# Expert loop: output weights fetched one expert ahead into a staging place and copied on by the vector engine

## The reference, cut to what matters

```python
def expert_block(args):
    xi, e = args
    hc = xi @ w1[e] + b1[e]                 # w1[e]: 1024 x 2048
    g, u = hc[:, :D_EXPERT], hc[:, D_EXPERT:]
    g = jnp.minimum(g, SWIGLU_LIMIT)
    u = jnp.clip(u, -SWIGLU_LIMIT, SWIGLU_LIMIT)
    hm = (u + 1.0) * (g * jax.nn.sigmoid(SWIGLU_ALPHA * g))
    return hm @ w2[e] + b2[e]               # w2[e]: 1024 x 1024
```

## Time and profile before

| | us |
|---|---|
| median of three runs | 2389.04 |
| the three runs | 2378.5, 2389.04, 2397.48 |
| the profiled execution | 2383.9 |
| its span | 2382.0 |
| PE busy | 2081.7 (87%) |
| DVE busy | 981.0 (41%) |
| ACT busy | 553.4 (23%) |
| POOL busy | 500.0 (21%) |
| DMA mean over the span | 329 GB/s |

### The profile page before, as it was taken

How to read it: one execution, slowest core, us unless ns; L and a number is a source line. 1 busy time by engine, 2 the same in 40 slices (tenths; PEclk the granted TensorE clock), 3 DMA queues, 4 the chain that set the end, 5 groups by cost and what they waited for, 6 DMA issues and landing times.

```text
span 2382.0 us, 27251 instructions
## 1 busy us (share of the span) xinstructions
PE 2081.7 (87%) x9038; PEld 1177.1 (49%) x9039; DVE 981.0 (41%) x2273; ACT 553.4 (23%) x1024; POOL 500.0 (21%) x562
## 2 busy tenths in 40 slices
PE   8998998957668577675899989999999999999998
PEld 7777887623223233232578854444444444444443
DVE  5955556547566566554275232211111111111112
ACT  4636301212112112121214222211111111112112
POOL 0000002466666666666200000000000000000000
PEclk9999999988788788897999989999999999999999
DMA  7352487799999999998743429799999999999996
GB/s 301 142 212 70 189 357 266 262 377 351 367 364 372 359 377 356 379 353 340 291 181 113 167 96 382 294 429 428 428 429 428 428 429 428 428 429 428 428 429 280
DMA packets 111703, 784.34 MB, mean 329 GB/s; under 512 B 13056, under 2 KB 13312, under 8 KB 80160
## 3 DMA queue, kind: packets, MB, share of 16 engines
q1 hardware_dynamic: 37920, 515.18, 52.2%
q0 software_dynamic: 73728, 268.47, 29.7%
HBM read 782.55 MB, written 1.05 MB: 329 GB/s over the span
## 4 chain that ended last, share of the span: by engine, by line
PE 71%; issue 12%; DVE 6%; POOL 3%; ACT 3%; DMA 2%; another core or an unknown queue 2%; DVEq 1%; POOLq 0%; ACTq 0%; SPq 0%
PE ps L779 57%; PE ps L938 11%; DVE ring L1932 2%; DMA arena<-in_peer_v,arena 2%; PE ps L1201 1%; POOL ring L739 1%; POOL ring L737 1%; PE ps L911 1%; DMA ring<-in_peer_v,arena 1%; ACT arena L1269 1%; DVE arena L1932 1%; DVE arena L1690 1%; DVE arena L1687 0%; DVE arena L1881 0%
## 5 line engine op out<-in xcount | busy, mean ns | idle before, releaser
L779 PE MATMUL ps<-ring,arena 128*64 128x512 f32 (+2 forms) x3336 | 749.6, 589 | 41.7 <-issue 41.7
L779 PEld LDWEIGHTS ps<-ring,arena 128*64 128x64 f32 (+1 forms) x3336 | 263.1, 140 | 501.2 <-issue 500.6
L938 PE MATMUL ps<-ring,arena 128*128 128x512 f32 x768 | 377.7, 649 | 147.3 <-issue 102.0
L779 PE MATMUL ps<-arena,ring 128*128 128x256 f32 (+1 forms) x2272 | 489.7, 375 | 3.8 <-DVE arena L1675 3.2
L779 PEld LDWEIGHTS ps<-arena,ring 128*128 128x128 f32 x2272 | 420.2, 190 | 66.7 <-issue 7.3
L938 PEld LDWEIGHTS ps<-ring,arena 128*128 128x128 f32 x768 | 157.8, 209 | 362.7 <-issue 309.2
L1932 DVE CUSTOM_DVE_ANT_0 ring<-ring,ps 128x1024 f32<-128x1024 f32 x192 | 228.6, 1218 | 105.9 <-DMA ring<-in_peer_v,arena 100.6
L938 PE MATMUL ps<-arena 128*128 128x512 f32 (+2 forms) x600 | 207.1, 594 | 69.9 <-ACT arena L1269 65.4
L1590 ACT COPY arena<-ps 128x512 f32<-128x512 f32 (+1 forms) x165 | 89.1, 540 | 739.7 <-PE ps L779 683.5
L2244 DVE TENSOR_TENSOR arena<-ps,arena 128x512 f32<-128x512 f32 x66 | 45.7, 692 | 438.7 <-PE ps L1201 438.7
L779 PE MATMUL ps<-arena 128*128 128x128 f32 (+4 forms) x1502 | 216.0, 299 | 9.3 <-ACT arena L1253 6.5
(11 more groups left out here) (336 smaller groups left out, 1214.8 us busy)
## 6 DMA issues: line engine op xcount, KB each, us to landing
ring<-in_w_exp SPq DMA_DIRECT2D x192, 2048.0 KB, 17.1
ring<-in_w_in SPq DMA_DIRECT2D x24, 2048.0 KB, 9.7
ring<-in_w_ada SPq DMA_DIRECT2D x12, 2048.0 KB, 9.0
ring<-in_w_out SPq DMA_DIRECT2D x4, 2048.0 KB, 8.4
ring<-in_w_peer_q SPq DMA_DIRECT2D x4, 2048.0 KB, 10.7
ring<-in_w_br_rnn SPq DMA_DIRECT2D x4, 1280.0 KB, 7.5
ring<-in_w_br_attn SPq DMA_DIRECT2D x2, 2048.0 KB, 14.3
ring<-in_peer_u,arena POOLq DMA_INDIRECT x192
```

The source lines that it names most:

```text
L779: return pe.matmul(o, l, r, start=start, stop=stop)
L938: return pe.matmul(o, l, r, start=start, stop=False, skip_group_check=True)
```

## The change

Ring and arena become two parts of one SBUF tensor (`words`), so that one instruction can address either by a register. Two staging places are laid over memory that is dead once the second block's `h3r` transposes are done. The output weights of expert e+1 are fetched into the staging places during expert e, each half under a semaphore of its own (`s_moved`), and the vector engine copies each half from staging to the ring after D of the pass before has been read. For a second pass of one expert the source is the ring place itself (`from_staged` holds 0), so that the copy moves data onto itself. Expert 0's output weights are loaded directly, expert 1's are staged before the loop. TensorE's D waits for the copy. After the loop the vector engine waits for the last copies. The units of the ring change their places (`place_of`), so that output weights lie at both ends.

```diff
--- before.py
+++ after.py
@@ -337,9 +337,9 @@
         def sem(name):
             return ctx.enter_context(nc.semaphore(name))
 
-        ring = ctx.enter_context(nc.sbuf_tensor("ring", [P, 6 * SLOT], F32))
         arena_words = 27400
-        arena = ctx.enter_context(nc.sbuf_tensor("arena", [P, arena_words], F32))
+        words = ctx.enter_context(nc.sbuf_tensor("words", [P, 6 * SLOT + arena_words], F32))
+        ring, arena = words[:, 0:6 * SLOT], words[:, 6 * SLOT:]
         ps = ctx.enter_context(nc.psum_tensor("ps", [P, N_BANKS, 512], F32))
         at = {"fixed": 0}
 
@@ -360,6 +360,7 @@
         ones = carve("fixed", P)
         cols = carve("fixed", N_COLS)
         eps = carve("fixed", 2)
+        staged_at = 6 * SLOT + at["fixed"]
         xT = carve("fixed", KD, T)
         hT = carve("fixed", KD, T)
         rstd = carve("fixed", T)
@@ -504,13 +505,19 @@
         of_pass = carve("M", 2, P)
         expert_of, part_of = of_pass[:, 0, :], of_pass[:, 1, :]
         last_of = carve("M", E)
+        from_staged = carve("M", P)
         assert at["M"] <= at["B"]
         g2_diag = carve("B", KD, P)
         assert at["B"] <= kept, (at["B"], kept)
         y_rows = ring[:, 0:TT * D].rearrange("p (a b) -> p a b", b=D)
         I32 = mybir.dt.int32
-        w1_unit = [ring[:, n * SLOT:(n + 1) * SLOT].rearrange("p (c j) -> p c j", c=KD) for n in range(4)]
-        w2_unit = [ring[:, n * SLOT:(n + 1) * SLOT].rearrange("p (c j) -> p c j", j=D) for n in (4, 5)]
+        place_of = {4: 0, 0: 1, 1: 2, 2: 3, 3: 4, 5: 5}
+        unit_words = [ring[:, place_of[n] * SLOT:(place_of[n] + 1) * SLOT] for n in range(6)]
+        w1_unit = [unit_words[n].rearrange("p (c j) -> p c j", c=KD) for n in range(4)]
+        w2_unit = [unit_words[n].rearrange("p (c j) -> p c j", j=D) for n in (4, 5)]
+        w2_start = [place_of[n] * SLOT for n in (4, 5)]
+        w2_staged = [words[:, staged_at + start:staged_at + start + SLOT] for start in w2_start]
+        assert at["M"] <= staged_at + w2_start[1] - 6 * SLOT <= kept - SLOT
 
         s_par = sem("params_loaded")
         s_x = [sem(f"x_loaded_{j}") for j in range(4)]
@@ -627,6 +634,7 @@
         s_g, s_sg = sem("expert_gate_ready"), sem("expert_sigmoid_ready")
         s_hm = sem("expert_hidden_ready")
         s_yg = sem("expert_rows_ready")
+        s_moved = [sem(f"staged_weights_moved_{half}") for half in range(2)]
         s_fin = sem("experts_done")
         s_y, s_yroot, s_yn = sem("y_ready"), sem("y_root_ready"), sem("y_normed")
         s_row = sem("rows_loaded")
@@ -664,9 +672,15 @@
                     sp.wait_ge(s_poolB, 1)
                     sp.dma_start(b2[0:E, :], a["b_exp_out"]).then_inc(s_smallw, 16)
 
-            def load(e, n):
-                sp.dma_start(ring[:, n * SLOT:(n + 1) * SLOT],
+            def load(e, n, to=None):
+                sp.dma_start(unit_words[n] if to is None else to,
                              a["w_exp"][bass.ds(e, 1), n].rearrange("e p w -> (e p) w")).then_inc(w_full[n], 16)
+
+            def stage(e, q=None):
+                for half in range(2):
+                    if q is not None:
+                        sp.wait_ge(s_moved[half], q + 2)
+                    load(e, 4 + half, w2_staged[half])
 
 
             n_second = len(units)
@@ -675,16 +689,25 @@
                     sp.wait_ge(s_mrg, 4 + 4)
                     load(0, 5)
                 unit_free(sp, last_in_slot(n, n_second))
-                load(0, n)
+                load(0, next(u for u in range(6) if place_of[u] == n))
+            B.filled(sp, "h3r", 3)
+            stage(1)
             sp.wait_ge(s_slots, 1)
             sp.dma_start(final_row, a["final_g"].partition_broadcast(P)).then_inc(s_row, 16)
-            with sp.Fori(1, E) as e:
-
-                q = sp.value_load(last_of[0:1, bass.ds(e - 1, 1)].bitcast(I32), min_val=0, max_val=MAX_PASSES - 1)
-                for job, ns in (("Zg", (0, 1)), ("Zu", (2, 3)), ("D", (4, 5))):
+            def last_pass(e):
+                return sp.value_load(last_of[0:1, bass.ds(e, 1)].bitcast(I32), min_val=0, max_val=MAX_PASSES - 1)
+
+            def first_weights(e, q):
+                for job, ns in (("Zg", (0, 1)), ("Zu", (2, 3))):
                     X.filled(sp, q, job)
                     for n in ns:
                         load(e, n)
+
+            with sp.Fori(1, E - 1) as e:
+                q = last_pass(e - 1)
+                first_weights(e, q)
+                stage(e + 1, q)
+            first_weights(E - 1, last_pass(E - 2))
             for t in range(TT):
                 sp.wait_ge(s_yn, t + 1)
                 sp.dma_start(out[t * P:(t + 1) * P, :], y_rows[:, t, :]).then_inc(s_out, 16)
@@ -1236,6 +1259,7 @@
                 for k in range(KD):
                     if k % 4 == 0:
                         pe.wait_ge(w_full[4 + k // 4], e * 16 + 16)
+                        pe.wait_ge(s_moved[k // 4], q + 1)
                     for half in range(2):
                         last = mm(ps[half * NS:(half + 1) * NS, EXPERT_BANK["D"], :],
                                   hm[:, k % 4, (k // 4) * NS:(k // 4 + 1) * NS],
@@ -2214,7 +2238,10 @@
                     own(dve.tensor_copy(last_of.bitcast(I32), count))
                 elif kind == "table":
                     B.filled(dve, *job)
-                    own(dve.tensor_copy(of_pass[0:E].rearrange("p a b -> p (a b)").bitcast(I32), ps[0:E, b, 0:2 * P]))
+                    own.mark(dve.tensor_copy(of_pass[0:E].rearrange("p a b -> p (a b)").bitcast(I32),
+                                             ps[0:E, b, 0:2 * P]))
+                    own(ts(from_staged[0:E], ps[0:E, b, P:2 * P], 0.5, float(staged_at), ALU.is_lt, ALU.mult))
+                    own(dve.tensor_copy(from_staged[0:E].bitcast(I32), from_staged[0:E]))
                     dve.sem_inc(free[b], 1)
                     dve.sem_inc(s_slots, 1)
                 elif kind == "gT":
@@ -2228,11 +2255,14 @@
             own(dve.tensor_copy(bias_now, b1[:, 0, :]))
             select(selg, 0, 0, True)
             dve.sem_inc(s_selg, 1)
+            for half in range(2):
+                dve.sem_inc(s_moved[half], 1)
             total = dve.value_load(total_i[0:1, 0:1].bitcast(I32), min_val=E, max_val=MAX_PASSES)
             with dve.Fori(0, total) as q:
                 own.enter(q, 2 + 6 + 1 + 2 + 1)
                 e = dve.value_load(expert_of[0:1, bass.ds(q + 1, 1)].bitcast(I32), min_val=0, max_val=E - 1)
                 part = dve.value_load(part_of[0:1, bass.ds(q + 1, 1)].bitcast(I32), min_val=0, max_val=3)
+                source = dve.value_load(from_staged[0:1, bass.ds(q + 1, 1)].bitcast(I32), min_val=0, max_val=staged_at)
                 dve.wait_ge(s_xg, q * 2 + 2)
                 select(sel, e, part, False)
                 dve.sem_inc(s_sel, 1)
@@ -2262,12 +2292,18 @@
                 own(tt(yg, ps[:, EXPERT_BANK["D"], :], g2_halves, ALU.mult))
                 dve.sem_inc(x_free[EXPERT_BANK["D"] - 4], 1)
                 dve.sem_inc(s_yg, 1)
+                for half in range(2):
+                    dve.wait_ge(w_full[4 + half], e * 16 + 16)
+                    dve.tensor_copy(unit_words[4 + half], words[:, bass.ds(source + w2_start[half], SLOT)])\
+                        .then_inc(s_moved[half], 1)
                 own.leave_open()
             end = Own(dve, s_vend)
 
 
             dve.wait_ge(s_fin, 1)
             dve.wait_ge(s_row, 16)
+            for half in range(2):
+                dve.wait_ge(s_moved[half], total + 1)
             halves = lambda x: x.rearrange("p (a b) -> p a b", b=512)
             end(tt(halves(y_rows[:, 1, :]), ps[:, 2:4, :], halves(final_row), ALU.mult))
             dve.sem_inc(s_y, 1)
```

## The result

The change made the kernel slightly slower, by less than one per cent: 2399.8 us in the median of 20 runs against 2390.98 of 20 runs before, ratio 1.0043 with a 95% interval of 1.0028 to 1.0058, which is 7 to 14 us. The forecast was 2395 (range 2377 to 2409), 6.35 us above before.

What follows compares the result with a forecast made beforehand. The expert loop was taken as bound by DMA bytes due before the last Zu. Terms 3.2 (later issue), 0.5 (front) and 2.65 (tail) sum to 6.35 us, on the median 2389.04 giving 2395 us, range 2377 to 2409.

Steps and rivals of the forecast that it cites:

- What bounds: Expert loop: DMA saturated at 428 GB/s, passes 29.36 us apart; the wait ending last is before Zu, not D.
- The count of bytes: From the DMA restart to u(31)'s landing: 28 output-weight pairs before and after, net 0 us where 9.8 could be expected.
- Rival A: Fetching ahead is worth one pair's transfer: loop ends 9.8 us sooner, whole time 2382 us; chance 0.12.
- The issue of w2: Output weights issued 3.2 us later, behind product and copy; paid once, at the first saturated expert, +3.2 us.
- The vector engine's time: Two copies a pass, 4.8 us with gaps, and a register load fit into 12.58 us of idle time: 0 us.
- In front of the loop: Two small vector operations before the signal that starts the loop: +0.5 us, bounds 0 and 0.8.
- The tail: After the last pass the final product waits for needless copies, 2.9 us later; a 0.25 us wait falls away: +2.65 us.
- Sum: Whole kernel: 3.2 + 0.5 + 2.65 = 6.35 us above the kernel before.
- Rival B: Each vector copy runs at the slow rate, 4.44 us, adding 12.9 us: 2402 us; chance 0.12.
- Rival C: Copies and arriving weights hold each other up, decisive once a pass's first copy takes over 5.8 us; slower; chance 0.05.
- price of a restart: When a dry DMA queue restarts, 0.54 us lost in the microsecond after the issue at 1525.33, at 197 GB/s.

Runs made afterwards that it cites:

- alternate: Changed kernel without copies, odd experts' output weights used where staged; ratio to the kernel before 1.0008, time from end of expert 0's Zu 952.75 us.
- direct_last: Changed kernel with the last expert's output weights loaded straight to the ring; ratio to the kernel before 1.0005, time from end of expert 0's Zu 957.31 us.
- switch_25: As alternate, but from expert 26 on output weights go out behind their own expert's other weights; ratio to the kernel before 0.9958.
- copy_thrice: Changed kernel with two further same-size copies ahead of each copy; time from end of expert 0's Zu 1070.44 us, 109 us above the change.
- skip_last: Changed kernel without the two copies of the last pass; time from end of expert 0's Zu 959.08 us, 2.4 us less than the change.
- copy_twice: Changed kernel with one further same-size copy ahead of each copy; time from end of expert 0's Zu 1009.39 us, 48 us above the change.

## Why the prediction was right

**What bounds.** Right. The wait stays before Zu and the saturated rate at 428 GB/s; the spacing of passes is 29.38 instead of 29.37. The DMA ends as the last Zu starts, as forecast (table of stretches, then timeline):

```profile
2362.00:2363.00 1.00, 0.00 (x0) 0.00 (x0) 0.00 (x0) 0.59 (x1) 0.00 (x0) 1.00 0.05 16
```
```profile
2363.49 7.09 PE L802 MATMUL ps<-words 128*64 128x512 f32 x32 [1.49 <-issue]
```

**The count of bytes, 28 pairs against 28, worth 0.** Right, and shown by alternate, which pays for no copies and gains 1.2. My reason for it was incomplete. I named the last Zu's bytes; direct_last took a pair out of that count and gained 1.8, not 9.8. The full reason is that before every Zu in the saturated loop the same number of bytes is due, and TensorE's own 27.64 us cap what any lead can give back per pass. Rival A's gain exists (switch_25 has 8.0 of the 9.8 us), but only for a kernel that gives the lead up five or six passes before the end.

**The issue of w2.** The size was nearly right, 3.46 instead of 3.2 (the gap before the copy is 0.42, not 0.26). The step that failed is the word once, "But once, at the first saturated expert". The same delay counts a first time at expert 2: the queue was dry after u(1), w2(2) stands ahead of g(2) and u(2), and u(2) misses its Zu. That pass is 1.6 us longer (29.25 against 27.64). Of the 3.46 us by which w2(2) goes out later, 1.9 are absorbed and 1.6 reach TensorE. The second pass of expert 2, from which my count started, lets the DMA catch up but gives TensorE nothing back.

**The vector engine's time.** Right: copies of 2.29 us, and no wait of TensorE for them in the changed kernel. In copy_thrice, with six copies a pass, the cover is used up.

**In front of the loop.** 0.4 measured, 0.5 expected.

**The tail.** 2.63 measured, 2.65 expected, shown by skip_last (2.4).

**Sum.** 0.4 + 1.6 + 3.5 + 2.63 = 8.1 us where 6.35 stood. The missing part is the term at expert 2. The medians differ by 8.8, the ratio gives 10.3 with an interval from 6.7 to 13.9, which holds 8.1 but not 6.35. The measured 2399.8 lies 4.4 us above the forecast of 2395.4: 1.9 because the median of 20 runs before is higher than that of the three that I had, 1.8 from the missing term, and the rest is within the scatter. The number held because the missing term is small against the range (2377 to 2409); the mechanism was right but for this one place.

**Rival B** is refuted by the copy's 2.29 us. **Rival C** did not come, since weights land at full rate beside the copies; but its threshold, a first copy of 5.8 us, was too high: two copies in a row, 4.6 us, already suffice. Its price of a restart, 0.54 us, was too low: copy_twice loses 2.55 at the one shown.

## What to carry to other kernels

When a queue is saturated, fetching something earlier only changes the order of the bytes. Ask what must have landed before the wait that ends last, and count it before and after; a lead in bytes turns into time only while the consumer's own pace is faster than the queue's, at the difference of the two per pass, so it has to be given up early enough before the end. A copy that frees a buffer adds its duration to the issue of the next transfer, which counts wherever the queue happens to be dry, and every such place must be looked for, not the first alone.

## What the runs showed of the hardware

The first matmuls of the loop ran slower in some executions of the same kernel. The group of 64 took 15.65 us in one execution of the kernel before and 13.95 in the other, and the granted clock of 1415 to 1420 was 0.87 in the first, after 0.50, the lower level of 1.2 GHz, in each of the microseconds 1413 to 1416. Ahead of it TensorE had been partly idle, at a granted clock of 0.54 in 1395 to 1405, where it was busy for 7.4 of 10 us. In the other execution it was partly idle too (7.0 of 10 us in 1405 to 1415, clock 0.66), and yet its clock was at 1.00 all through 1415 to 1430, where its first Zg lies; what decides between the two is not shown.

A restart of a dry queue does not begin at full rate: 229 and 295 GB/s in the first two microseconds with data after the issue at 1538.07, and 213, 328 and 147 in three microseconds of one in copy_twice. From the issue into the empty queue at 1538.07 to the first data it took about 1 us.
